# Splitting each 512-column dense matmul of a hybrid retention / gated DeltaNet block into two of 256 columns

## What is computed

```python
mod = jax.nn.silu(c) @ ada_w[l] + ada_b[l]
shift_a, scale_a, gate_a, shift_m, scale_m, gate_m = jnp.split(mod, N_MOD, axis=-1)
h = modulate(rmsnorm(x, norm_mix_w[l]), shift_a, scale_a)
proj = (h @ w_in[l]).astype(f32)                    # 1024 -> 4104
mixed = token_mix(proj, ...)                        # 4 retention heads, 4 gated DeltaNet heads
x = x + gate_a[:, None, :] * (mixed @ w_out[l])     # 1024 -> 1024
h = modulate(rmsnorm(x, norm_mlp_w[l]), shift_m, scale_m)
x = x + gate_m[:, None, :] * (jnp.square(jax.nn.relu(h @ w_ff1[l])) @ w_ff2[l])
return rmsnorm(x, norm_final_w)                     # 1024 -> 4096 -> 1024 above
```

## Time and profile before

| what | value |
|---|---|
| time, median of 2 runs | 2845.03 us (2839.68 to 2850.39) |
| profiled execution, span from the first to the last instruction | 2846.2 us |
| mean granted TensorE clock | 0.994 |
| PE busy | 2777.8 us, 98% of the span, 14048 matmuls |
| PEld busy | 2335.5 us, 82%, 14048 loads |
| DVE / ACT / POOL busy | 1403.6 / 1094.1 / 1675.0 us |
| DMA | 109 GB/s over the span |

### The profile page before, as it was taken

One profiled execution on the slowest core, in us unless ns is written; L12 is line 12 of the kernel. 1 busy time (PEld: TensorE's weight loads), 2 busy tenths in 40 slices (PEclk: granted clock), 3 DMA queues, 4 the chain that ended last, 5 costly groups with the idle time before them and its releaser, 6 DMA issues.

```text
span 2846.2 us, 37200 instructions
## 1 busy us (share of the span) xinstructions
PE 2777.8 (98%) x14048; PEld 2335.5 (82%) x14048; DVE 1403.6 (49%) x1990; ACT 1094.1 (38%) x1895; POOL 1675.0 (59%) x1260
## 2 busy tenths in 40 slices
PE   5999999999999999999999999999999999999998
PEld 4788888878888888888888888888888888888886
DVE  5867665464647455553445436553353543322233
ACT  3533333343334434343344433343333333443332
POOL 3755554565566756575555756676565556665653
PEclk9999999999999999999999999999999999999999
DMA  7334344322333324322232323422222224233242
GB/s 274 112 126 145 133 149 159 116 102 91 108 115 116 107 75 132 105 86 86 83 121 93 111 73 102 145 78 93 78 89 78 86 78 141 91 99 99 90 127 88
DMA packets 98098, 311.64 MB, mean 109 GB/s; under 512 B 11520, under 2 KB 11520, under 8 KB 95872
## 3 DMA queue, kind: packets, MB, share of 16 engines
q1 hardware_dynamic: 67248, 246.85, 27.0%
q10 hardware_dynamic: 30672, 62.40, 6.7%
HBM read 285.09 MB, written 24.12 MB: 109 GB/s over the span
## 4 chain that ended last, share of the span: by engine, by line
PE 89%; DVE 5%; POOL 2%; issue 1%; ACT 1%; DMA 1%; ACTq 0%; SPq 0%; DVEq 0%; POOLq 0%
PE acc L491 25%; PE acc L493 25%; PE acc L492 24%; PE pm L526 8%; PE pm L531 2%; DVE mixing L1222 1%; POOL w L1644 1%; POOL mT L1653 1%; PE pm L625 1%; DMA mixing<-in_ada_w 1%; ACT io L766 1%; PE pm L655 1%; PE pm L630 1%; PE pm L581 0%; PE pm L626 0%
## 5 line engine op out<-in xcount | busy, mean ns | idle before, releaser
L1644 POOL TENSOR_TENSOR w<-raw,w 128x512 fp32r<-128x512 f32 x832 | 1136.9, 1369 | 1014.1 <-ACT w L737 1011.9
L737 ACT ACTIVATE w<-raw 128x512 fp32r<-128x512 f32 x832 | 520.7, 627 | 779.1 <-PE acc L493 728.2
L491 PE MATMUL acc<-mT,w 128*128 128x512 f32 x1536 | 625.2, 407 | 7.5 <-DVE mT L1538 3.3
L493 PE MATMUL acc<-mT,w 128*128 128x512 f32 x1536 | 601.6, 392 | 0.0
L492 PE MATMUL acc<-mT,w 128*128 128x512 f32 x1536 | 600.2, 391 | 0.0
L491 PE MATMUL acc<-hid,w 128*128 128x512 f32 x864 | 351.2, 406 | 2.7 <-DVE ffs L1438 1.4
L491 PEld LDWEIGHTS acc<-mT,w 128*128 128x128 f32 x1536 | 290.4, 189 | 64.4 <-issue 4.8
L493 PEld LDWEIGHTS acc<-mT,w 128*128 128x128 f32 x1536 | 289.3, 188 | 63.0
L493 PE MATMUL acc<-hid,w 128*128 128x512 f32 x864 | 337.7, 391 | 0.0
L492 PE MATMUL acc<-hid,w 128*128 128x512 f32 x864 | 336.8, 390 | 0.0
L492 PEld LDWEIGHTS acc<-mT,w 128*128 128x128 f32 x1536 | 290.6, 189 | 53.1 <-issue 1.0
(11 more groups left out here) (223 smaller groups left out, 3670.4 us busy)
## 6 DMA issues: line engine op xcount, KB each, us to landing
raw<-in_w_all SPq DMA_DIRECT2D x416, 512.0 KB, 3.5
ada_late<-in_ada_w SPq DMA_DIRECT2D x32, 512.0 KB, 5.1
xr<-in_xT ACTq DMA_DIRECT2D x48, 256.0 KB, 3.4
mixing<-in_ada_w SPq DMA_DIRECT2D x8, 1024.0 KB, 9.9
proj_kept<-ffs ACTq DMA_DIRECT2D x32, 256.0 KB, 2.1
out<-io ACTq DMA_DIRECT2D x32, 256.0 KB, 2.5
mixed_kept<-mixing ACTq DMA_DIRECT2D x28, 256.0 KB, 2.0
xr<-mixed_kept ACTq DMA_DIRECT2D x28, 256.0 KB, 2.8
```

What stands on the lines that cost most here:

```text
L491: e.matmul(bank, whi, x[:, 0, :], start=first, stop=False)
L493: m = e.matmul(bank, wlo, x[:, 0, :], start=False, stop=last)
L737: e.activation(w2[:, 0, local % HALVES, :], raw[:, tile % NRAW, local % 2 * NT:(local % 2 + 1) * NT], ACT.Copy).then_inc(S["w_hi"], 1)
L1644: e.tensor_tensor(w2[:, 1, local % HALVES, :], raw[:, tile % NRAW, local % 2 * NT:(local % 2 + 1) * NT], w2[:, 0, local % HALVES, :].bitca ...
```

## The change

Each of the three 512-column matmuls of a dense step becomes two of 256 columns. The three products of the left 256 tokens come first, then the three of the right 256. Only the very first matmul of a group, on the left half, keeps `start`; the right half's first matmul is issued without it into columns of the same bank. The `w_used` increment stays on the last matmul, now that of the right half.

```diff
@@ -488,9 +488,11 @@
                 at = k % 4
                 whi = w2[:, 0, slot, at * P:(at + 1) * P]
                 wlo = w2[:, 1, slot, at * P:(at + 1) * P]
-                e.matmul(bank, whi, x[:, 0, :], start=first, stop=False)
-                e.matmul(bank, whi, x[:, 1, :], start=False, stop=False)
-                m = e.matmul(bank, wlo, x[:, 0, :], start=False, stop=last)
+                for c in (slice(0, NT // 2), slice(NT // 2, NT)):
+                    e.matmul(bank[:, c], whi, x[:, 0, c], start=first and c.start == 0, stop=False,
+                             skip_group_check=True)
+                    e.matmul(bank[:, c], whi, x[:, 1, c], start=False, stop=False, skip_group_check=True)
+                    m = e.matmul(bank[:, c], wlo, x[:, 0, c], start=False, stop=last, skip_group_check=True)
                 if k % 4 == 3:
                     m.then_inc(S["w_used"], 1)
```

## The result

The changed kernel takes 2945.06 us (2944.89 to 2945.23, 2 runs) against 2845.03 us before: 3.5% slower, ratio 1.035, 95% interval 1.0303 to 1.0397. The profiled execution has a span of 2943.1 us and a time of 2944.9 us. The range of the prediction (2840 to 2990) holds it, but only because the range was drawn to take in the rivals: its likeliest case, no measurable change at 2860 us, didn't come. The time lies beside the rival of late loads (2935 us).

The account below looks back on a forecast made before the run. TensorE's dense matmuls were taken to bound the kernel (79% of the span). To the 2846.2 us span came 15 us for added starts and 0 for loads, waits and instructions: 2861 us, median 2860, range 2840 to 2990.

Parts of the forecast that it names:

- likeliest case: Dense matmuls: the 13 ns belong to the columns and loads fit; 2860 us, own range 2840 to 2885; 54 in 100.
- rival of late loads: Dense halves wait for their weight loads, some 9 ns once per old matmul: +90 us, 2935 us; 16 in 100.
- The clock of the changed kernel: TensorE's clock: 2.4 GHz assumed for the dense matmuls; the forecast would be wrong if it fell.
- hand-overs: Waits between TensorE, POOL and ACT around the dense groups: no wait added, cost 0.
- additional instructions: TensorE's issue of 48064 matmuls and loads instead of 28096: cost 0.
- what these 13 ns belong to: Dense matmuls' 13.0 ns beyond their columns, per column or per instruction: 0 to +130 us, taken as +15 us.
- The load fits beneath it with 2 ns to spare: Weight loads in dense steps: a 111 ns load is hidden beneath a 113.2 ns half matmul.
- I take 0 for it: The 9984 additional weight loads of the dense steps, hidden beneath half matmuls: cost 0.
- rival of fixed cost: Each of 9984 added dense matmul starts pays 13 ns: +130 us, 2975 us, 4.6% slower; 26 in 100.
- What would show it: Signs in dense stretches: 113 to 115 ns confirms the forecast, 120 fixed cost, alternating 113 and 122 or trailing loads late loads.

Follow-up runs that it names:

- the run with 4 x 128: Each 512-column dense matmul of the kernel before the change became four of 128 columns, with full 128-column weight loads: 5811.97 us, ratio 2.039.

## Why the prediction was right or wrong

- **TensorE's dense stream sets the time, and a nanosecond there goes in whole: right.** Its starts account for 96.6 us of the 96.9 by which the span grew; other starts took 0.1 us less.
- **The clock of the changed kernel, the hand-overs and the additional instructions cost nothing: right.** Mean clock 0.995; POOL waited 1114.2 us for ACT and ACT 788.2 for PE, longer than before; and 9984 added matmuls and loads cost nothing at all when the loads are short (ratio 1.0002).
- **Two halves by themselves cost what the whole did: right on the sum, on a wrong ground.** The step "what these 13 ns belong to" had to choose between columns and instruction, and took 1.5 ns for each added start. With short loads the halves run at 113.3 ns, twice that is 226.7, so the added start cost nothing. But the 13 ns are neither the one nor the other: 6.7 ns at 128 and at 256 columns with short loads, 12 to 15 at 320 and 384, 13 to 20 at 512. Taking the cost of an added `fp32r` start from the float32 matmul of rows 7 was too much. Rows 8 did not bear on it at all: 110 and 111 ns is the pace of full loads, the same 111.6 that `fp32r` matmuls of 128 columns have in the run with 4 x 128, and no row shows that transposes move at half the column rate.
- **"The load fits beneath it with 2 ns to spare" and "I take 0 for it": here the likeliest case failed.** I compared the 111 ns between two loads with the 113.2 of half a matmul as if each ran alone. With full loads each half came 6.7 ns later: 19968 x 6.7 = 133 us, of which 97 stayed. With loads of half the width nothing was lost. That the stated range still holds the time is owed to the rivals in it, not to this term, and the 54 in 100 for no measurable change were on the wrong side.
- **The rival of late loads** named the place and the condition. Its size came by accident: I took some 9 ns at every second matmul (90 us); it was 6.7 ns at every one, less what came back. Its picture of a load that finishes a fixed time before its matmul is also not what the runs show, and the 114 to 120 ns that it read from rows 9 and 10 were not the load's: the first dense distance behind small products, 314 ns, is 315 with a load of 16 columns.
- **The rival of fixed cost** has the right distance, 120 ns, and the wrong reason; by its own words in "What would show it" I would have called it right. Only the short loads told the two apart.
- **What I did not foresee: 36.6 us came back.** About half of it is in the middle of dense work, where the distances had been stretched beyond 226.7 ns before (mean 228.2) and are a little below 120 now (119.7).
- The 2.5 ns that the Trainium skill gives for a start in an isolated, warm gap ("TensorE: Matmul & The Clock Gate", section "Back-to-back issue gap") would have given +25 us; measured were +97 us with full loads and 0 with short ones, so it matches neither. The Trainium skill's advice ("Perfetto Trace Analysis", section "Identifying the Most-Contended Engine") to look at the arithmetic done and the busy share of weight loads, and not at the busy share of matmuls, fits: matmuls were 98% busy in both, loads went from 82 to 97%.

**What stays open.** Shown is that in rows of 256-column matmuls the cost needs weights of more than 64 columns, that it is complete at 128, and that order, the count of starts and a repeated load don't matter. Not shown is what couples the two, and not even that the thin cover is the reason: 320-column matmuls have 30 ns of cover and the same 12 to 13 ns over their columns, and no run has short loads at 320 or 384 columns. Not shown either: why a uniform row of halves settles at 120 ns when mixed with whole ones they come at 115, why whole ones then go from 227 to 233, and why shorter loads make 512-column matmuls slower. All distances look like the columns plus a few steps of some 7 ns that fall differently with the pattern; that is a description and not a cause. Whether loads and moving columns meet in SBUF was not tried.

## What to carry to other kernels

A weight load that is hidden with room beneath a 512-column matmul may not be free beneath one of 256 columns, when its own length is nearly the same: compare the two with a margin, and expect a few per cent where only 2% is left between them. Of the splits tried here with all products computed, none was as fast as the unsplit 512 columns, which fill a PSUM bank; at 128 and 192 columns the load alone sets the pace (111 to 113 ns each). To find whether a cost is the start's or the load's, shorten the load and keep the starts. And before pricing a single distance, add up a whole repeating pattern: the recorded start of a matmul can stand before its load is done.

## What the runs showed of the hardware beyond that

- With full loads and 128 columns the granted clock fell to 0.50 for 1400 us in one piece, although TensorE issued without a gap before it fell; the time doubled rather than growing by the 76% that was estimated for the loads at full clock (5010 us).
- A shorter weight load made the unsplit kernel slower, by 0.4 to 0.5% with 16 and with 112 of 128 columns (intervals 1.0018 to 1.0063 and 1.0032 to 1.0066).
- In the long dense stretches late in the trace the distance with full loads is strikingly constant, 226 or 227 ns at 512 columns (699 of 706 from 2480 to 2640 us) and 120 ns at 256; earlier, between small products, with another load length or with a mix of lengths, it wanders over some 10 ns.
